# Three buffers for weight blocks and six for expert rows, in place of two and seven

## The reference

```python
def peer_ffn(h, w_query, sub_keys, u_tab, v_tab):
    q = (hf @ w_query).reshape(M, H, 2, PEER_DQ // 2)
    s = jnp.einsum('mhpc,hpnc->mhpn', q, sub_keys)
    top_s, top_i = lax.top_k(s, K)                  # 16 of 128 keys, twice a head
    ...                                             # the 16 best sums of 16 x 16 pairs
    ids = jnp.take_along_axis(cand_i, best_c, axis=-1)
    g = jax.nn.softmax(best_s, axis=-1)
    u = jnp.take(u_tab, idb, axis=0)                # 128 rows a token
    v = jnp.take(v_tab, idb, axis=0)
    act = jax.nn.gelu(jnp.einsum('nkd,nd->nk', u, xb)) * gb
    return jnp.einsum('nk,nkd->nd', act, v)

for layer in range(2):
    h = h + mixer[layer](rms_norm(h, mix_norm[layer]))
    h = h + peer_ffn(rms_norm(h, ffn_norm[layer]), ...)
return rms_norm(h, final_norm)
```

## Time and profile before

| what | value |
|---|---|
| median of 3 runs | 2921.01 us (2920.56 to 2922.98) |
| the profiled execution's own time | 2919.51 us |
| its span, first to last instruction | 2917.7 us |
| PE busy | 2259.3 us, 77% |
| DVE busy | 1905.1 us, 65% |
| ACT busy | 1275.8 us, 44% |
| POOL busy | 987.6 us, 34% |
| moved by DMA | 1183.52 MB, mean 406 GB/s over the span |
| mean granted TensorE clock | 0.848 of full speed |

### The profile page before, as it was taken

One profiled execution on the slowest core, in us unless ns is written; L12 is line 12 of the kernel. 1 busy time (PEld: TensorE's weight loads), 2 busy tenths in 40 slices (PEclk: granted clock), 3 DMA queues, 4 the chain that ended last, 5 costly groups with the idle time before them and its releaser, 6 DMA issues.

```text
span 2917.7 us, 36442 instructions
## 1 busy us (share of the span) xinstructions
PE 2259.3 (77%) x12132; PEld 887.7 (30%) x12132; DVE 1905.1 (65%) x5678; ACT 1275.8 (44%) x3758; POOL 987.6 (34%) x1028
## 2 busy tenths in 40 slices
PE   8999987778996877787786877867877666766666
PEld 6764333223452322232331322323332111111110
DVE  2358656777478867576677667576578666467544
ACT  3244543585435456334344437334434333335333
POOL 0023333333333333333333333333333333333332
PEclk9999999898997978888997887988998766666666
DMA  6379999999999999999999999999999999999998
GB/s 258 108 311 426 426 426 426 426 419 427 421 406 413 425 424 422 427 417 426 426 423 412 426 426 415 426 425 421 426 421 418 415 427 427 427 415 423 427 427 338
DMA packets 167100, 1183.52 MB, mean 406 GB/s; under 512 B 19568, under 2 KB 20096, under 8 KB 24192
## 3 DMA queue, kind: packets, MB, share of 16 engines
q0 software_dynamic: 147456, 1073.81, 87.9%
q1 hardware_dynamic: 19456, 107.39, 9.1%
HBM read 1179.03 MB, written 2.10 MB: 405 GB/s over the span
## 4 chain that ended last, share of the span: by engine, by line
DMA 47%; PE 27%; DVE 13%; ACT 8%; issue 5%; POOL 0%; DVEq 0%; SPq 0%; POOLq 0%; ACTq 0%
DMA main_ring<-in_uv,main_idi 47%; PE main_bank L372 13%; PE main_bank L416 7%; DVE main_ring L298 6%; PE main_bank L414 3%; ACT main_diagonal L315 2%; ACT main_act_out L311 1%; ACT L303 1%; ACT main_act_out L303 1%; DVE main_idf L208 1%; DVE main_topi L161 1%; DVE main_work L153 1%; PE main_bank L664 1%; DVE main_topi L155 1%; DVE main_top L150 0%
## 5 line engine op out<-in xcount | busy, mean ns | idle before, releaser
L372 PE MATMUL main_bank<-main_ring,main_diagonal 64*64 64x512 f32 x8192 | 1380.0, 759 | 611.9 <-ACT main_diagonal L315 569.4
L298 DVE CUSTOM_DVE_ANT_0 main_ring<-main_ring,main_bank 128x1024 f32<-128x1024 f32 x1024 | 1242.0, 1219 | 840.5 <-DMA main_ring<-in_uv,main_idi 812.3
L281 POOL DMA_INDIRECT main_ring<-in_uv,main_idi x1024 | 987.4, 964 | 1905.9 <-PE main_bank L372 1701.4
L303 ACT ACTIVATE main_act_out<-main_hid 128x1 f32<-128x1 f32 x1024 | 206.8, 202 | 1422.0 <-DVE main_hid L298 1401.8
L372 PEld LDWEIGHTS main_bank<-main_ring,main_diagonal 64*64 64x64 f32 x8192 | 254.7, 153 | 1408.4 <-ACT main_diagonal L315 1221.8
L416 PE MATMUL main_bank<-main_xT,main_w_block 128*128 128x256 f32 x1408 | 406.7, 417 | 11.8 <-ACT main_xT L850 8.3
L315 ACT ACTIVATE main_diagonal<-main_ones,main_act_out 128x64 f32<-128x64 f32 x1024 | 356.2, 348 | 34.3 <-PE main_bank L372 0.6
L416 PEld LDWEIGHTS main_bank<-main_xT,main_w_block 128*128 128x128 f32 x1408 | 252.5, 197 | 299.6 <-issue 259.7
L311 ACT ACTIVATE main_act_out<-main_act_out,main_gate 128x1 f32<-128x1 f32 x1024 | 301.6, 295 | 33.3
L416 PE MATMUL main_bank<-main_xT_query,main_w_block 128*128 128x256 f32 x448 | 115.6, 397 | 0.0
L414 PE MATMUL main_bank<-main_w_block,main_xT 128*128 128x256 f32 x384 | 100.5, 398 | 0.0
(11 more groups left out here) (230 smaller groups left out, 1316.2 us busy)
## 6 DMA issues: line engine op xcount, KB each, us to landing
main_w_block<-in_w_query SPq DMA_DIRECT2D x32, 1024.0 KB
main_w_block<-in_w_ab SPq DMA_DIRECT2D x24, 1024.0 KB
main_ring<-in_uv,main_idi POOLq DMA_INDIRECT x1024
main_w_block<-in_w_c_in SPq DMA_DIRECT2D x16, 1024.0 KB
main_w_block<-in_w_c_out SPq DMA_DIRECT2D x8, 1024.0 KB
main_att_bias<-in_att_bias SPq DMA_DIRECT2D x16, 256.0 KB
main_ring<-in_w_out SPq DMA_DIRECT2D x4, 1024.0 KB, 5.0
main_w_block<-in_w_out SPq DMA_DIRECT2D x4, 1024.0 KB
```

Source lines behind the costliest of these rows:

```text
L281: nc.gpsimd.indirect_dma_start(self.ring[n % self.bufs], None, self.uv[p // NT], bass.IndirectOffsetOnAxis(self.choice.idi[:, p % 2, k:k + ...
L298: self.nc.vector.tensor_tensor_reduce(out=row, in0=row, in1=self.ps[:, 6:8], scale=1.0, scalar=0.0, op0=ALU.mult, op1=ALU.add, accum_out=s ...
L303: self.nc.scalar.activation(self.act_out[:, k:k + 1], self.hid[:, k:k + 1], ACT.Gelu_apprx_tanh).then_inc(self.gelued, 1)
L372: last = self.nc.tensor.matmul(self.ps[a * SIDE:(a + 1) * SIDE, 4 + r], self.diagonal[rows, n % DIAGS], self.ring[n % self.bufs][rows, D + ...
```

## The change

The ring of expert rows gets six slots in place of seven, the weight blocks get three buffers in place of two, and the four blocks of the opening's output projection sit in ring slots 2 to 5 in place of 3 to 6. A ring slot and a weight block both take 8 KB of each partition, so the memory in use is the same. No instruction is added or removed; only the numbers that the waits of POOL and SP use, and the addresses, differ.

```diff
-BUFS = 7
+BUFS = 6
...
     HEADS = 2
-    HELD = 3
+    HELD = 2
...
-        wbuf = room.sb("w_block", [P, 2, KD * BC])
+        wbuf = room.sb("w_block", [P, 3, KD * BC])
...
-        weights = Weights(nc, s, [wbuf[:, k] for k in range(2)], bank)
+        weights = Weights(nc, s, [wbuf[:, k] for k in range(3)], bank)
```

## The result

The changed kernel takes 2932.08 us (median of 6 runs, 2930.78 to 2936.8) against 2920.74 us (6 runs) before, +11.3 us; the ratio is 1.004, with a 95% interval of 1.003 to 1.005. Its profiled execution has a span of 2929.0 us. The prediction said 2950, range 2919 to 2982: slower was right, but the forecast of +29 us is more than twice what was measured.

The account below looks back on a forecast made before the run. From about 162 us on, time is bytes divided by the DMA rate. 2919.5 - 2.5 (moved load) + 2.5 (opening's ring) + 29 (late releases with six slots) = 2948.5, plus 1.5 to the median: 2950 us, range 2919 to 2982.

Parts of the forecast that it names:

- The opening: Before the gathers fill the DMA engines: moved weight load -2.5 us and one gather less +2.46 us cancel to 0.
- the moved block: Weight block 14's load goes out before 160 us instead of at 179.47, into idle DMA time: -2.5 us.
- the lost gather: In the opening, the seventh gather waits for step 0, so one gather less is in before a DMA hole: +2.46 us.
- the reserve of six slots: How late a release may be before the DMA engines idle: 4.2 us with seven slots, 1.8 with six.
- the break-even distance: Distance between two gathers that the reserve covers: 6.6 us with seven slots, 4.2 with six; 71 distances exceed 4.2.
- the way on an empty queue: Issue to dot of a gather on a drained queue, read from the gather of 180.78: 8.4 us.
- the first rival: Six slots are enough, not slower: fixed part of issue to dot under about 6.5 us; 2921 us, chance 0.19.
- the subtraction: Calm issue to dot, 12.65 us, less 8.4 on a drained queue gives 4.2 us of reserve with seven slots.
- The factor 0.3: Share of late-release cost paid in passes 0 to 5, from five dips at 17 distances: 0.3 x 73.7 = 22 us.
- six slots are enough: Rival: the reserve counted as lost is only queueing, so six slots keep 3.7 us; 2919 to 2922 us, chance 0.19.
- Calm rate not held: Rival: with six slots each calm gather takes 2.53 us, 0.08 more, over some 900 gathers; 2990 us, chance 0.12.
- The third buffer gives more than it takes: Rival: weight loads running a block earlier fill DMA holes at late releases; gain 6.5 us at most, 2914, chance 0.04.

Follow-up runs that it names:

- r6w2: Six slots with two weight buffers, against the kernel before with seven slots: 2932.58 us against 2922.73, ratio 1.0033.
- six2: Six slots with two weight buffers, measured again beside the changed kernel: 2929.52 us against 2921.59 for the kernel before, ratio 1.0025.
- r7held: Kernel before, seven slots and two buffers, with the fourth to sixth gathers waiting for one more product each: 2919.20 us against 2921.59, ratio 0.999.
- r5w3: Five slots, HELD 1, three weight buffers, against the kernel before: 3063.35 us against 2922.73, ratio 1.0485.
- stall7: Kernel before, seven slots, with five delays of idle ACT copies (128 x 1024) in calm steps of passes 6 and 7: cost 1.2 us.
- light7: Kernel before, seven slots, with 11 of 16 matmuls of each of pass 1's query products left out: 2921.03 us, ratio 0.9996.
- big7: Kernel before, seven slots, with 4 to 8 longer idle ACT copies (128 x 1408) in calm steps of passes 6 and 7: cost 7.1 us.

## Why the prediction was right in its sign and wrong in its size

The bound was right in the main. From 182 us to the end the time is bytes by rate, and two thirds of what makes it longer stand in windows where the DMA engines are partly idle. Where the rest comes from stays open. In the changed kernel, too, PE never waited for a weight block.

The opening: by the bytes moved up to 250 us, its sum was -2.5 and not 0. Windows from 0 to 250 us, before and then after:

```profile
0.00:250.00 250.00, 233.42 (x1290) 172.92 (x1290) 108.26 (x433) 91.12 (x235) 29.42 (x35) 0.99 0.64 251
0.00:250.00 250.00, 233.93 (x1302) 172.76 (x1303) 111.21 (x441) 93.62 (x241) 28.78 (x35) 1.00 0.64 255
```

The changed kernel is 1.1 MB ahead there, the moved block. r6w2 and six2, with two buffers, have 250 and 249 GB/s, and their first gather started 0.7 and 1.1 us later than before, which is that difference: the lost gather cost nothing. The reason is that step 0 was done sooner than before. The seventh gather, which waits for it, went out at 178.03, where the eighth had gone out at 180.78. The last product of the output projection began 1.2 us sooner and took 3.72 us in place of 5.31, as r7held shows too with seven slots. The prediction has no row of it. But the moved block's 2.5 us is in no median: the changed kernel then loses some 14 us in the full stretch, where those with two buffers lose 8 to 10.

**The step that failed** is the reserve of six slots, 1.8 us, and with it the break-even distance of two gathers, 4.2 us, which gave the +29 us. The delays put the reserve at about 3.2 us and the break-even at 5.7: 23 distances exceed that, where the prediction priced 71.

Two things in it were mis-sized, and in opposite directions. The first is the way on an empty queue: "A gather issued on a drained queue, that of 180.78, has its dot at 189.16: 8.4 us." That queue was not drained. SP's load of block 14 went out at 179.47, 1.3 us ahead of the gather. Delays in the last passes, where no weight is loaded, give 5.5 and 5.7 us; that the load's megabyte makes the difference fits, and was not tried by itself. I had this cause in hand in the first rival ("since a weight load ran beside the gather of 180.78") and priced that rival with 6.5 us, but gave it 0.19. The second is the subtraction. With 5.6 in place of 8.4 it gives a reserve of 7.0 us with seven slots and 4.6 with six, more than the delays found (4.8 and 3.2, or 5.7 and 2.9 the other way). So the calm way less the empty way overstates the reserve here, and that made good part of the error in the 8.4.

Put right, the sum comes close, by luck. In the kernel before, the excess over 5.7 us, at most 2.46 us each, sums to 27.6 us in passes 0 to 5 and 2.5 in passes 6 and 7. With the covered share left as it was, that is 0.3 x 27.6 + 2.5 = 10.8 us. With seven slots the break-even is about 7.2, which ten distances exceed, by 4.7 us in all; less 1.5 us for those, six slots should cost 9.3 us, against 11.3 measured. But pass by pass it doesn't hold. The rule gives 1.3 us in passes 0 and 1 together, where the dots of the changed kernel fall back by 12.3, 4.0 in passes 3 and 5, where they gain 2.5, and 2.5 in passes 6 and 7, where they lose nothing.

The factor 0.3 was weak from the start. Five dips of the share were set against 17 distances over 6.5 us, but of the five only the one at 1596 lies at such a distance (7.3 us). Near 584, 1764 and 2232 the longest is 5.5 to 5.9 us, and from 867 to 881, at pass 1's end, none is over 3.8. That suggests that a run of slightly late gathers can empty the queue, which a rule for single distances doesn't see. Passes 6 and 7 without cover were priced at 6.8 us and cost 0. The lower end of the range's sum names eight places and multiplies by seven.

With five slots the fitted reserve is 1.5 us, a break-even of 4.0: 86 distances in the kernel before exceed that. That shows why the next slot costs so much more; the rule's most, 92 us, is still under the 131.

The rivals: "six slots are enough" had its mechanism right in part and its time wrong by 11 us. "Calm rate not held" was wrong for six slots (2.48 us apart in both) and is part of what happens with five (2.53). "The third buffer gives more than it takes" is refuted: with six slots it gives nothing to the time, or harm; with seven it was not tried.

The Trainium skill's rule ("DMA: Bandwidth & Descriptors", Anatomy of one DMA: 2.0 us and the bytes at 436 GB/s, by which I had estimated 4.4 us) lies 1.1 us under the 5.5 us measured here from issue to dot; my 8.4 lay 2.9 over. By its 4.4 us, four slots would do, as an estimate. Five already cost 141 us over before, so the rule was nearer for one gather and still misleads for the depth of a ring, which also has to hold the releases that come late.

What stays open: how much of the loss belongs to the third buffer (3.8 us in one pair, none in the other), why late releases cost so much in passes 0 and 1 and nothing in 6 and 7, and where the third of the loss goes that stands in windows with a full share.

## What to carry to other kernels

A ring in front of a saturated transfer queue is priced by its reserve, which is at most the slots times the transfer's time, less the way of one transfer from issue to release on an empty queue. Here that gives 7.0 and 4.6 us for seven and six slots, and delays put in on purpose found about 5 and 3. Each slot taken costs more than the one before (here 11 us, then 131). Take the empty-queue time only from a transfer with no other queue at work beside it, or provoke one with a delay in a calm stretch, and read from the trace how long the delay really was. Check a price not only by its sum but by where in the run the time is lost. And a deeper buffer for an operand that is never late bought nothing here.

## What the runs showed that I had not expected

With a shorter ring the fastest way from issue to dot in normal work also fell: the shortest of all 1024 was 7.1 us with seven slots, 5.7 with six (the changed kernel) and 5.2 with five (r5w3). So the 7.1 us of the seven slots were not a fixed latency.

The last product of the opening's output projection (L664) is slower in the kernel before than in r7held and in all kernels with fewer slots. Before, it took 5.31 us and the first dot started at 176.64; in r7held, with the gathers held back, 3.72 us and 175.41. The rows of the product, before and then r7held:

```profile
168.34 5.31 PE L664 MATMUL main_bank<-main_ring,main_mixT 128*128 128x256 f32 x16 [2.82 <-DVE main_resid L672]
```

```profile
168.70 3.72 PE L664 MATMUL main_bank<-main_ring,main_mixT 128*128 128x256 f32 x16 [1.71 <-DVE main_resid L672]
```

PE waited 2.82 us for DVE before the first and 1.71 us before the second, and the granted clock differs. Windows of 168 to 174 us, before and then r7held (the clock is the third number from the end):

```profile
168.00:174.00 6.00, 5.66 (x20) 4.61 (x20) 2.87 (x7) 0.10 (x2) 0.58 (x2) 0.72 1.00 416
```

```profile
168.00:174.00 6.00, 4.71 (x25) 4.04 (x26) 4.36 (x14) 1.42 (x4) 1.63 (x3) 1.00 1.00 392
```

Before, the clock is at 1.2 GHz from 168.2 to 171.6 us (0.72 on average over the window), in r7held at 2.4 GHz throughout. At half the clock those 3.4 us do 1.7 us less of work, which is the product's 1.6 us. The other kernels with seven slots and the opening as it was (stall7, light7, big7) have such a stretch at 1.2 GHz at the same product, and none with six or five slots has it. Whether DVE came later because of the gathers, or by something else in their order, was not tried.
